# Norm sums of squares: seven tiles added on VectorE, two partition sums on TensorE in place of eight

## The reference

```
def rms_norm(x, g):
    xf = x.astype(jnp.float32)
    y = xf * lax.rsqrt(jnp.mean(xf * xf, axis=-1, keepdims=True) + EPS)
    return (y * g.astype(jnp.float32)).astype(x.dtype)
...
x = x + gate1[:, None, :] * mix
h = modulate(rms_norm(x, norm2_g[l]), shift2, scale2)
x = x + gate2[:, None, :] * swiglu(h, ffn_w_gate[l], ffn_w_up[l], ffn_w_down[l])
```

## Time and profile before

| | us |
|---|---|
| median of 3 runs | 2411.8 |
| lowest and highest of the 3 | 2411.66, 2414.57 |
| the profiled execution, device time | 2414.91 |
| its span, first to last instruction | 2413.1 |
| TensorE busy in the span | 2249.8 |
| VectorE busy in the span | 1090.3 |
| ScalarE busy in the span | 848.8 |

### The profile page before, as it was taken

One profiled execution on the slowest core, in us unless ns is written; L12 is line 12 of the kernel. 1 busy time (PEld: TensorE's weight loads), 2 busy tenths in 40 slices (PEclk: granted clock), 3 DMA queues, 4 the chain that ended last, 5 costly groups with the idle time before them and its releaser, 6 DMA issues.

```text
span 2413.1 us, 29168 instructions
## 1 busy us (share of the span) xinstructions
PE 2249.8 (93%) x11006; PEld 1728.1 (72%) x11006; DVE 1090.3 (45%) x1583; ACT 848.8 (35%) x1310; POOL 24.5 (1%) x29
## 2 busy tenths in 40 slices
PE   4687899999998789999999999999999998999997
PEld 2443668887866556888888777676888876888885
DVE  4783345444356664534324444555424334333332
ACT  4432332222245464423223344552222223322222
POOL 2100000000000000000000000000000000000000
PEclk8798999999999799999999999999999999999998
DMA  8477545545421003233233212222333322333331
GB/s 286 169 268 283 188 136 200 187 157 186 137 80 56 6 19 97 70 107 111 72 113 106 78 53 62 60 54 54 96 96 96 96 82 67 96 107 88 97 103 58
DMA packets 360891, 269.97 MB, mean 112 GB/s; under 512 B 20402, under 2 KB 346400, under 8 KB 350544
## 3 DMA queue, kind: packets, MB, share of 16 engines
q1 hardware_dynamic: 345548, 250.00, 33.6%
q10 hardware_dynamic: 15236, 18.50, 2.5%
HBM read 265.39 MB, written 3.08 MB: 111 GB/s over the span
## 4 chain that ended last, share of the span: by engine, by line
PE 82%; DVE 7%; ACT 3%; DVEq 2%; DMA 2%; issue 2%; ACTq 1%; SPq 0%; POOL 0%; POOLq 0%
PE G L526 59%; PE G L2072 9%; PE MS L1402 1%; PE AD L409 1%; DVE tb L606 1%; PE MS L2301 1%; DMA ada_s<-in_ada_w 1%; PE X L2282 1%; DMA TTall<-in_s_b_im 1%; PE X L2548 1%; DVE scan L761 1%; PE X L1814 1%; DVE wlo L512 1%; DVEq L605 1%; ACT whi L506 1%
## 5 line engine op out<-in xcount | busy, mean ns | idle before, releaser
L512 DVE TENSOR_TENSOR wlo<-raw,whi 128x1024 fp32r<-128x1024 f32 (+1 forms) x296 | 380.8, 1287 | 930.3 <-ACT whi L506 927.3
L506 ACT ACTIVATE whi<-raw 128x1024 fp32r<-128x1024 f32 (+1 forms) x296 | 328.1, 1109 | 904.8 <-PE G L526 757.4
L526 PE MATMUL G<-Ahi,whi 128*128 128x512 f32 x1440 | 573.3, 398 | 16.7 <-DVE Alo L611 9.3
L526 PE MATMUL G<-Ahi,wlo 128*128 128x512 f32 x1440 | 563.8, 392 | 0.0
L526 PE MATMUL G<-Alo,whi 128*128 128x512 f32 x1440 | 563.6, 391 | 0.0
L526 PEld LDWEIGHTS G<-Ahi,whi 128*128 128x128 f32 x1440 | 272.2, 189 | 89.4 <-issue 20.2
L526 PEld LDWEIGHTS G<-Ahi,wlo 128*128 128x128 f32 x1440 | 272.4, 189 | 58.6 <-issue 3.4
L526 PEld LDWEIGHTS G<-Alo,whi 128*128 128x128 f32 x1440 | 272.2, 189 | 57.4
L526 PE MATMUL G<-mhi,whi 128*128 128x512 f32 x528 | 211.8, 401 | 0.0
L526 PE MATMUL G<-mlo,whi 128*128 128x512 f32 x528 | 205.7, 390 | 0.0
L526 PE MATMUL G<-mhi,wlo 128*128 128x512 f32 x528 | 205.4, 389 | 0.0
(11 more groups left out here) (511 smaller groups left out, 2669.0 us busy)
## 6 DMA issues: line engine op xcount, KB each, us to landing
ada_s<-in_ada_w SPq DMA_DIRECT2D x40, 1024.0 KB, 8.0
raw<-in_w_in SPq DMA_DIRECT2D x64, 512.0 KB, 4.1
ada_ff<-in_w_ada SPq DMA_DIRECT2D x24, 1024.0 KB, 6.2
raw<-in_ffn_w_gate SPq DMA_DIRECT2D x44, 512.0 KB, 3.9
raw<-in_ffn_w_up SPq DMA_DIRECT2D x44, 512.0 KB, 3.9
raw<-in_ffn_w_down SPq DMA_DIRECT2D x32, 704.0 KB, 4.7
raw<-in_w_ffn_in SPq DMA_DIRECT2D x44, 512.0 KB, 3.8
raw<-in_w_ffn_out SPq DMA_DIRECT2D x16, 704.0 KB, 4.7
```

Of the source, the lines that this page charges most:

```text
L506: last = E.eng.activation(whi[j][:, k0:k0 + k, 0:c], raw[j][:, k0:k0 + k, 0:c], ACT.Copy)
L512: last = E.eng.tensor_tensor(wlo[j][:, k0:k0 + k, 0:c], raw[j][:, k0:k0 + k, 0:c], whi[j][:, k0:k0 + k, 0:c].bitcast(FP32), ALU.subtract)
L526: mm = E.eng.matmul(out_, a[j][:, k0 + kk, 0:c], b(kk), start=first and kk == 0 and n == 0, stop=last and kk == k - 1 and n == 2)
```

## The change

VectorE keeps a running sum of squares in `rstd`. It clears the tile ahead of each of the six phases (a memset), and behind the update of tile n (n = 0 to 6) it waits for ScalarE's square of that tile and adds it (`sum_squares`). TensorE has no product of squares inside a phase any more. Behind the phase it waits until the seven adds are done (`sq_free`), multiplies the ones by `rstd`, runs `fill[0]`, waits for the square of tile 7, adds its product, and runs `fill[1]`. With fewer products to set apart, one pair of tiles is written out ahead of TensorE's loop where two were.

```
             squares = ph in ENDS
-            per = {"sq_ready": 2} if squares else {}
...
-                    if squares and not (peeled and first == 0):
-                        if peeled and j == 0:
-                            E.eng.wait_ge(S("ms_done"), E.nth("ms_done"))
-                        add_squares(E, j, first=peeled and j == 0)
...
-            peel = 2 if squares else 1 if gradual or second else 0
+            peel = 1 if gradual or second else 0
...
             if squares:
-                add_squares(E, 0)
+                E.eng.wait_ge(S("ms_done"), E.nth("ms_done"))
+                E.eng.wait_ge(S("sq_free"), SQ0[ph] + 2 + 7)
+                E.eng.matmul(MS[:, :], ones, rstd[:, :], start=True, stop=False)
                 if fill:
                     fill[0]()
-                add_squares(E, 1, last=True)
+                E.eng.wait_ge(S("sq_ready"), E.nth("sq_ready", 8))
+                E.eng.matmul(MS[:, :], ones, sq[1][:, :], start=False, stop=True).then_inc(S("sq_free"), 1)
                 if fill:
                     fill[1]()

-        def add_squares(E, j, first=False, last=False):
-            E.eng.wait_ge(S("sq_ready"), E.nth("sq_ready"))
-            E.eng.matmul(MS[:, :], ones, sq[j][:, :], start=first, stop=last).then_inc(S("sq_free"), 1)
+        def sum_squares(E, ph, n, j, u):
+
+            if not (isinstance(n, int) and n == TILES[ph] - 1):
+                E.eng.wait_ge(S("sq_ready"), n + (SQ0[ph] + 1))
+                E.eng.tensor_tensor(rstd[:, :], rstd[:, :], sq[j][:, :], ALU.add).then_inc(S("sq_free"), 1)
...
                 E.eng.tensor_tensor(x, x, tb[j][:, :], ALU.add).then_inc(S("tb_used"), 1)
                 E.eng.drain().then_inc(S("x_tile"), 1)
+                sum_squares(E, "glu", n, j, u)
+            E.eng.memset(rstd[:, :], 0.0)
             phase(E, "glu", low_part, work)
...
                 if ph in ENDS:
                     E.eng.drain().then_inc(S("x_tile"), 1)
+                    sum_squares(E, ph, n, j, u)
+            if ph in ENDS:
+                E.eng.memset(rstd[:, :], 0.0)
             phase(E, ph, low_part, work, hooks)
```

More of the change, by code:

```diff
@@ L93 @@
 ENDS = ("glu", "dn1", "wo", "dn3", "mix", "dn5")
-ORDER = [p[0] for p in PHASES]
+SQ0 = {"glu": 1, "dn1": 9, "wo": 21, "dn3": 29, "mix": 37, "dn5": 45}
 TILES = {p[0]: p[1] for p in PHASES}
@@ L1386, in phase_pe @@
                     pair(0, n, True)
-                with E.loop(TILES[ph] // 2 - peel, **per) as i:
+                with E.loop(TILES[ph] // 2 - peel) as i:
                     pair(i, peel, False)
```

## The result

| | before | after |
|---|---|---|
| median, us | 2411.97 | 2386.16 |
| lowest and highest of 4 runs | 2411.66, 2414.57 | 2383.83, 2387.80 |
| the profiled execution, device time | 2414.91 | 2386.81 |
| its span | 2413.1 | 2385.0 |

The ratio of the medians is 0.9892, with a 95% interval from 0.9877 to 0.9908: 25.8 us less. The prediction was 2389.5 with a range from 2384 to 2394, so 22.3 us less.

A forecast was written before the change was run, and what follows sets the result against it. TensorE was taken as the bound, busy in 93% of the span with 82% of the chain of waits. Four norms' 17.2 us, "dn5" 4.35 and "wo" 0.8 sum to 22.3: from 2411.8 to 2389.5 us, range 2384 to 2394.

The forecast's parts named there:

- Five products on the chain for a norm: In each norm, five removed products of squares stood between tiles on TensorE's chain, 0.86 us each: 4.3 us a norm.
- The sixth product: Behind the last tile: gives nothing in "glu", "dn1", "dn3", "mix"; counts in "wo", where all six make 5.15 us.
- The new wait in "wo": Behind the last tile of "wo", TensorE waits 2.5 us for the seventh add, leaving 2.65 of 5.15 us.
- The clock behind it: Behind the wait in "wo" the granted clock falls and 1.85 us are lost, so "wo" gives 0.8 us.
- rival (a): "wo" keeps its clock: the gap comes, the loss doesn't; 24.15 us saved, 2387.7 us; chance 0.25.
- Gaps elsewhere: TensorE's gaps behind the last tile grow to 1.9 us in "glu", 2.9 in "mix"; cost taken: nothing, bounds 0 to 0.9 each.
- rival (c): Grown gaps in "glu" and "mix" each slow the last product by 0.9 us: 20.5 us saved, 2391.3 us; chance 0.13.
- The adds: 42 adds on VectorE, 693 ns each, 29 us in all, delay no split; 1.3 us stay free in "glu".
- (b): "wo" doesn't wait at all, its hooks running 2.5 us earlier: 26.7 us saved, 2385.1 us; chance 0.06.
- (d): TensorE's stream has slack, 28% of the removed time being free anyway: 16.1 us saved, 2395.7 us; chance 0.04.
- (e): No change: the tiles are paced by something else and the gaps only grow; 2411.8 us; chance 0.03.
- (f): Slower: VectorE's adds stand serially on the splits' path, costing 61 us against 27 removed; 2446 us; chance 0.03.

## Why the prediction was right

**Five products on the chain for a norm: right, and 0.04 us short.** The chain gave 0.86 us for a product. The tiles are in fact spaced 0.90 us closer: 5 x 0.90 is the 4.50 us found up to the last tile in "glu", "dn1", "mix" and "dn5" ("dn3" has 4.42). With the product a tile took 5.48 + 0.86 = 6.34 us; without it VectorE's splits below start 5.44 us apart. So the tile behind a product had cost 0.04 us more than one behind a tile, and the product's own duration leaves that out. Over six norms that is 1.2 us.

**The sixth product: right in four norms, wrong as a rule for "wo".** In "glu", "dn1", "dn3" and "mix" its removal only widened TensorE's gap, as argued. For "wo" I counted it, since filler covers the norm there. The moved hooks show what the filler hid: with the wait gone, TensorE waits 0.77 us for the square of tile 7, and "wo" gives 4.4 us, not 5.15. In the changed kernel itself the product does count, because the wait for the add is last: 5.15 - 2.48 = 2.67 us, which is what the first trace has.

**The new wait in "wo": right.** 2.5 us predicted, 2.48 and 2.51 measured, ended by the seventh add, with `c0lo` ahead of it on the chain.

**The clock behind it: right in two runs of three.** The step took the loss of 1.85 us as certain. It came in two of three traces with that wait (both of the changed kernel, and the one with work in the gap of "mix"), with about 1.5 us, and left "wo" at 1.17 and 1.29 us where it came and at 2.67 where it didn't. Forecast and rival (a) are the two outcomes of one kernel, and a sum that books the loss in full is 1.5 us off where it doesn't come, at 2.48 us of idle time and a clock of 1.00. The row that the step went by, the slow tile at 941.29, is itself there in only two of the five traces of before.

**Gaps elsewhere, rival (c): half right.** At 1.69 us in "glu" the product was fast in all seven traces with that gap. At 2.92 us in "mix" it was slow in three of five, with 0.85 us each time, where the rival had 0.9. The row of 2.06 us without a loss was no ground for taking nothing at 2.9.

**The adds: right.** 692 ns for 693, no tile and no product on `rstd` late outside "wo". VectorE's rows ahead of the last three splits in "glu" give the room left:

```profile
285.21 1.23 DVE L512 TENSOR_TENSOR wlo<-raw,whi 128x1024 fp32r<-128x1024 f32 x1 [1.02 <-ACT whi L506]
...
290.65 1.23 DVE L512 TENSOR_TENSOR wlo<-raw,whi 128x1024 fp32r<-128x1024 f32 x1 [1.18 <-ACT whi L506]
...
296.09 1.23 DVE L512 TENSOR_TENSOR wlo<-raw,whi 128x1024 fp32r<-128x1024 f32 x1 [1.34 <-ACT whi L506]
```

1.0 to 1.3 us, where 1.3 was worked out. A small cost that I hadn't seen: "dn1" gives 4.14 us and not 4.50, because behind its root the chain holds 0.44 us of issue on VectorE where before had 0.06:

```profile
685.30 0.05 DVEq L605
685.35 0.44 issue
```

That is in all traces of changed kernels but the one with tripled adds, and its cause is open. It cancels the 0.36 us ahead of "dn5".

**The other rivals.** (b), no wait in "wo", is refuted by the wait itself. (d), slack in the stream, would have given 0.72 of each product; four norms gave more than the whole, so the 28% in which no weight load ran were no room that these products could have used. (e), no change, falls with it. (f), the adds serial with the splits, did not happen; its point of decision did lie where it was put, a little over 1 us away, but what happens beyond it was wrong. I had the lateness enter each tile and add 61 us. Tripled adds, 1.5 us longer, cost 13: weights split two tiles ahead let it pile up in "glu" and come out once, behind the last tile, and in "wo" at tile 6 and behind the last.

**The size.** 25.8 us against 22.3. 1.0 to 1.7 us of the difference lie in the norms (products worth 0.90 us, and "wo" above its term, less "dn1" and in one trace the loss in "mix"). About 2 us lie outside, where the traces of one kernel differ by more than that, and remain open. That the time lies in the range shows less than the stages do. In the changed kernel's first trace "wo" came out as in rival (a) and "mix" as in rival (c), in the second "wo" with the forecast's loss and "mix" without one, and the range held both. That the two sums differ by 0.65 us only is chance. A slip in the working: the chances of the cases that are faster add up to 0.93, not 0.94.

## What to carry to other kernels

- Count a removed operation only where it stands on the chain: here five of eight products of a norm, and a sixth only where another wait covers the end. Price it by the spacing of its neighbours with and without it, not by its own duration.
- When work moves to an engine with time to spare, look for the place where that engine has other work as well; there the new wait is (here 2.5 us in one of six). Splits made two tiles ahead let an engine that was late by up to 2 us get by until the end of "glu", and charged it there; in "wo", where it was later, a tile had to wait.
- Before a forecast is compared with one trace of before, take a second and a third: stretches that no edit touches differed here by up to 5.6 us.

## What the hardware showed besides

- The same gap in the same kernel, 2.5 us of idle TensorE in a stream otherwise full, was followed by a granted clock of 0.58 in one run and of 1.00 in another. No single length of gap divides the two: products with the ones behind 2.45 and 2.92 us were fast at times, one behind 1.98 us was slow, and above 3 us all five were, at least in part. At one place with the same work around it, tile 2 of "wo", 1.71 us and less left the clock up in five of five traces, and 1.78 to 1.99 us brought it down in eight of nine.
- An fp32 product of 128 x 512 with a 128 x 128 matrix, two weight loads and two matmuls, costs a full stream 0.90 us. Behind a gap its two matmuls take 1.1 us at the upper clock level, and 2.0 to 2.1 at the lower.
- Where the clock falls in the attention stage is another draw: the five traces of one kernel had the falls at different places, and their spans ran from 2406.3 to 2413.1 us.
